# Moving a layer's second expert choice into the next window, and making the samples' input projections with the prompt's weight tiles

## What is computed

```python
mod = (silu(c) @ w_ada + b_ada)                    # 6 x 1024 per sequence
h = rms_norm(x, norm1_g) * (1 + sc1) + sh1
qa, ka, va, qb, kb, vb, zb, bb, ab, qc, kc, vc = split_cols(h @ w_in, IN_SPLITS)   # 1024 x 3592
o_a = window attention (three dilations);  o_b = gated DeltaNet with a causal conv over qb, kb, vb
o_c = stick-breaking attention (samples: over a paged cache)
x = x + gt1 * (concat(o_a, o_b, o_c) @ w_out)
h2 = rms_norm(x, norm2_g) * (1 + sc2) + sh2
q = (h2 @ wq); s = scores against 128 + 128 product keys, 8 heads
top 16 of each half, top 16 of the 256 sums -> 128 experts and gates per token
x = x + gt2 * sum over the 128 experts of gate * gelu(h2 . u_tab[i]) * v_tab[i]
```

## Time and profile before

| | us |
|---|---|
| median of three runs | 4719.75 (4712.13 to 4724.38) |
| profiled execution, its own time | 4694.12 |
| its span in the profile | 4692.3 |
| PE, DVE, ACT, POOL busy | 3425.7, 2843.8, 877.2, 2587.5 |
| moved by DMA | 1401.71 MB, 1107.44 of it by POOL's gathers |

### The profile page before, as it was taken

One profiled execution on the slowest core, in us unless ns is written; L12 is line 12 of the kernel. 1 busy time (PEld: TensorE's weight loads), 2 busy tenths in 40 slices (PEclk: granted clock), 3 DMA queues, 4 the chain that ended last, 5 costly groups with the idle time before them and its releaser, 6 DMA issues. The chain is left out here.

```text
span 4692.3 us, 42307 instructions
## 1 busy us (share of the span) xinstructions
PE 3425.7 (73%) x11982; PEld 1910.2 (41%) x11982; DVE 2843.8 (61%) x5777; ACT 877.2 (19%) x2045; POOL 2587.5 (55%) x2244
## 2 busy tenths in 40 slices
PE   5966768539298889575887967498898436748897
PEld 2624543126154554262455426255553113213351
DVE  1225552556866648787774688868649767584322
ACT  1113110011142112112321211242221011000120
POOL 0000362025767757687774667777656767665563
PEclk8986789759589999796998988799999767869896
DMA  6451375549989989899998889999988989999995
GB/s 229 139 180 56 101 227 177 187 104 320 354 318 345 385 308 339 331 399 342 366 376 320 306 334 395 353 346 361 367 306 308 378 303 348 362 382 377 336 330 154
DMA packets 586674, 1401.71 MB, mean 299 GB/s; under 512 B 67314, under 2 KB 287659, under 8 KB 585244
## 3 DMA queue, kind: packets, MB, share of 16 engines
q0 software_dynamic: 306176, 1107.44, 63.6%
q1 hardware_dynamic: 261836, 274.77, 17.7%
q10 hardware_dynamic: 18432, 16.79, 1.1%
HBM read 1387.11 MB, written 11.88 MB: 298 GB/s over the span
## 5 line engine op out<-in xcount | busy, mean ns | idle before, releaser
L2496 PE MATMUL bank<-arena 128*128 128x512 f32 (+1 forms) x3264 | 1589.6, 636 | 200.5 <-PEq L2493 117.9
L2392 POOL DMA_INDIRECT arena<-in_peer_u_dram,arena x1056 | 1279.6, 1212 | 693.2 <-issue 303.1
L2392 POOL DMA_INDIRECT arena<-in_peer_v_dram,arena x1056 | 1160.5, 1099 | 749.2 <-PE bank L2496 448.4
L2442 DVE CUSTOM_DVE_ANT_0 arena<-arena 128x1024 f32<-128x1024 f32 (+1 forms) x1056 | 1269.8, 1224 | 447.5 <-DMA arena<-in_peer_u_dram,arena 417.4
L2496 PEld LDWEIGHTS bank<-arena 128*128 128x128 f32 (+1 forms) x3264 | 614.8, 196 | 1013.6 <-issue 869.5
L2479 ACT ACTIVATE arena<-arena 128x128 f32<-128x128 f32 (+1 forms) x816 | 301.5, 394 | 1072.9 <-PE bank L2496 686.1
L2458 DVE SCALAR_TENSOR_TENSOR arena<-arena 128x1024 f32<-128x1024 f32 x232 | 297.6, 1283 | 243.6 <-DMA arena<-in_peer_v_dram,arena 223.3
L799 PE MATMUL bank<-arena 128*128 128x256 f32 (+3 forms) x1472 | 368.9, 414 | 101.0 <-PEq L792 95.9
L2138 POOL DMA_INDIRECT arena<-in_cache_sb_k_dram,arena x64 | 84.0, 1312 | 550.4 <-POOLq L2131 530.2
L799 PEld LDWEIGHTS bank<-arena 128*128 128x128 f32 (+1 forms) x1472 | 247.0, 170 | 220.8 <-issue 156.1
L641 PE MATMUL bank<-arena 128*9 128x512 f32 x384 | 180.3, 627 | 66.9 <-PEq L637 45.9
(11 more groups left out here) (339 smaller groups left out, 3730.0 us busy)
## 6 DMA issues: line engine op xcount, KB each, us to landing
arena<-in_w_in_dram SPq DMA_DIRECT2D x78, 1024.0 KB, 13.2
arena<-in_w_ada_dram SPq DMA_DIRECT2D x24, 2048.0 KB, 8.4
arena<-in_w_out_dram SPq DMA_DIRECT2D x24, 1024.0 KB, 13.0
arena<-in_peer_wq_dram SPq DMA_DIRECT2D x24, 1024.0 KB, 15.0
arena<-in_peer_u_dram,arena POOLq DMA_INDIRECT x1056, 7.4
arena<-in_peer_v_dram,arena POOLq DMA_INDIRECT x1056, 6.2
arena<-in_cache_sb_k_dram SPq DMA_DIRECT2D x128, 128.0 KB
arena<-in_cache_sb_v_dram SPq DMA_DIRECT2D x128, 128.0 KB
```

Source lines behind the costliest of these rows:

```text
L2392: pool_.indirect_dma_start(G_[g % GR][0:b.parts, :], None, tables[0 if which == "u" else 1], bass.IndirectOffsetOnAxis(ap=b.index[:, n:n + ...
L2442: vec.tensor_tensor_reduce(row, row, b.h, 1.0, 0.0, ALU.mult, ALU.add, b.AV[0:b.parts, n:n + 1]).then_inc(freed_by_dve, 1)
L2496: last = pe_.matmul(ps[6 + i][0:b.rows, :], DG[owners[g][1] % NDG][0:b.parts, 0:b.rows], G_[g % GR][0:b.parts, i * GBLK:(i + 1) * GBLK], s ...
```

## The change

1. The second `choose_tile` of each unit leaves the lane. It becomes a program of its own, `second_choice`, in the next window at positions 0 to 0.22, that is, in front of the u blocks of tile b. With it gone, layer 1's modulation is no longer in two halves: 24 chunks of 256 columns (tiles of 1 MB, a ring of four) stand beside the one choice left, which is paced 80 there and 59 elsewhere.
2. In a window's last value phase, where v blocks have no u blocks beside them, DVE takes every second row from row 8 on (`ON_DVE_ALONE = 2`): 60 of 128. Elsewhere it stays at one in four.
3. The samples have no projection of their own. The prompt's `project` takes the eight sample rows along: the convolution's matmuls are 264 columns wide in place of 256, and each of the eight other tiles gets a group of eight matmuls for the samples. Layer 0's go with unit 0 straight to the samples' buffers. Layer 1's go with unit 3, in the fourth window, by way of small stores to a DRAM tensor, from where `rows_back` fetches them in the last window; the convolution's features wait in the tile H2S. The samples' norm stands at the head of the sample lane (layer 0) or of the prompt lane (layer 1).
4. In the first window the samples' lane is the norm at positions 0 to 0.02, the rest of layer 0's modulation at 0.02 to 0.25, and from 0.255 the other stages, behind a wait for the prompt's projection. In the last window it spans 0 to 0.8 in place of 0.85. `delta_sample` has three ticks more, in which PE transposes the features to rows for the output.

```diff
+ON_DVE_ALONE = 2
...
-    return not b.sample and n >= FIRST_ON_DVE and n % ON_DVE == ON_DVE - 1
+    return not b.sample and n >= FIRST_ON_DVE and n % b.every == b.every - 1
...
+            for phase in phases:
+                for which, b in phase:
+                    if which == "v":
+                        b.every = ON_DVE_ALONE if len(phase) == 1 else ON_DVE
...
-            def project(u, m):
+            def project(u, m, s=None):
...
-                        mine = [(c, kind, i) for i in range(nt)]
+                        mine = [(c, kind, i) for i in range(nt)] + ([(c, kind, "sample")] if s else [])
...
+                        if spill and t - 2 in of_samples:
+                            k = of_samples.index(t - 2)
+                            lo, hi, _ = CHUNKS[groups[t - 2][0]]
+                            sp_.wait_ge(act2sp, 1).then_inc(act2sp, -1)
+                            sp_.dma_start(ROWS[:, lo:hi], s.m.STAGE[k % 3][:, 0:hi - lo]).then_inc(k_landed[k % 3], 16)
...
-                                    last = pe_.matmul(ps[t % BANKS][:, 0:n_], m.W[c % ring][:, k, off:off + P], m.HT[:, k, 0:n_],
+                                    last = pe_.matmul(ps[t % BANKS][:, 0:wide], m.W[c % ring][:, k, off:off + P], m.HT[:, k, 0:wide],
                                                       start=(k == 0), stop=(k == KD - 1))
+                                elif i == "sample":
+                                    last = pe_.matmul(ps[t % BANKS][0:NB, 0:hi - lo], m.HT[:, k, n_:wide],
+                                                      m.W[c % ring][:, k, 0:hi - lo], start=(k == 0), stop=(k == KD - 1))
...
                                 act_.copy(m.BT[:, f, 3:3 + n_], bank[:, 0:n_]).then_inc(act2dve, 1)
+                                if s is not None:
+                                    act_.copy(s.m.BF[:, f, :], bank[:, n_:wide])
...
+                                if out_to_dram and k >= 3:
+                                    act_.wait_ge(k_landed[k % 3], 16).then_inc(k_landed[k % 3], -16)
...
+                        if spill and t == ticks - 1:
+                            for k in range(len(of_samples) - 3, len(of_samples)):
+                                act_.wait_ge(k_landed[k % 3], 16).then_inc(k_landed[k % 3], -16)
...
+            def rows_back(u, m):
+
+                def sp():
+                    for dst, lo, hi in ((m.PZ[0:NB, 0, :], 2304, 2816), (m.BA[0:NB, 0, :], 2816, 2824), (m.QKC[0:NB, 0, :], 2824, 3336),
+                                        (m.VC[0:NB, 0, :], 3336, 3592), (m.QKA[0:NB, 0, :], 0, 512), (m.VA[0:NB, 0, :], 512, 768)):
+                        sp_.dma_start(dst, ROWS[:, lo:hi]).then_inc(loaded, 16)
+                    yield
+                    sp_.wait_ge(loaded, 96).then_inc(loaded, -96)
+                    yield
...
-                    return [paced(begin, 8), paced(project(u, m), 80), paced(heads(u, m), 14)] + between + [paced(delta_sample(u, m), 75),
+                    return [paced(heads(u, m), 14), paced(delta_sample(u, m), 80),
...
-                return [paced(begin, 14), paced(project(u, m), 102), paced(unit_lengths(u, m), 31), paced(heads(u, m), 19),
+                begin = norm(u, 0, m.H1, m.HT, m.SEG, m.SQJ, m.SMALL, first_w)
+                before = [paced(sample_norm(s.u, m, m.HT), 8)] if s is not None and s.normed is None else []
+                return before + [paced(begin, 14), paced(project(u, m, s), 120 if s else 102), paced(unit_lengths(u, m), 31), paced(heads(u, m), 19),
...
-                        paced(choose_tile(u, e, 0, meanwhile[0:1]), 59), paced(choose_tile(u, e, 1, meanwhile[1:2]), 59)]
+                        paced(choose_tile(u, e, 0, meanwhile), 80 if meanwhile else 59)]
...
+        def second_choice(u, span):
+
+            ticks, programs = LC.choose_tile(u, None, 1)
+            return [span[0] + (span[1] - span[0]) * (n + 1) / ticks for n in range(ticks)], programs
...
-        tiles = [AR.room(KD, GBLK) for _ in range(2)]
-        late = [LP.modulate(1, tiles, GBLK, half * MOD // 2, (half + 1) * MOD // 2) for half in range(2)]
+        late = [LP.modulate(1, [AR.room(KD, GBLK // 2) for _ in range(4)], GBLK // 2)]
...
+        rest_of_samples = [paced(LS.after_lane(LP, LP.walked + 2), 2)] + LS.token_mixers(samples[0], rooms[0])
+        window(LP.token_mixers(units[0], m, own, late),
+               [([paced(LS.sample_norm(samples[0], rooms[0][0], m.HT), 8)], 0.0, 0.02), ([paced(rest, 50)], 0.02, 0.25), (rest_of_samples, 0.255, 1.0)], [])
...
+            choice = second_choice(u, (0.0, 0.22))
             if k < 3:
-                window(LP.token_mixers(units[k + 1]), [], phases)
+                own = None
+                if k == 2:
+                    own = Room()
+                    own.u, own.m, own.normed = samples[1], rooms[1][0], None
+                window(LP.token_mixers(units[k + 1], prompt_room(units[k + 1]), own), [], phases, choice)
...
+                of_sample = [paced(LS.rows_back(samples[1], rooms[1][0]), 4)] + LS.token_mixers(samples[1], rooms[1])
+                window([], [(of_sample, 0.0, 0.8)], phases + [[("u", s)], [("v", s)]], choice)
```

More of the change, by code:

```diff
@@ L163 @@
 ON_DVE = 4
+W_IN = 3592
+ON_DVE_ALONE = 2
 FIRST_ON_DVE = 8
@@ L485, in sample_room @@
             m.DB = AR.room(CONV_CH)
+            m.BF = AR.room(CC, NB) if u.l == 0 else H2S[:, 0:CC * NB].rearrange("p (c b) -> p c b", c=CC)
+            m.STAGE = None if u.l == 0 else [H2S[0:NB, CC * NB + i * (CW_ + 8):CC * NB + (i + 1) * (CW_ + 8)] for i in range(3)]
             rest = AR.at
-            m.HT = AR.room(KD, NB)
-            m.W = [AR.room(KD, CW_ + 8) for _ in range(4)]
             ends = [AR.at]
@@ L745, in project @@
                 tap = {i: f for f, i in feature_at.items()}
-                BANKS = 2 if u.sample else 4
+                of_samples = [i for i, g in enumerate(groups) if g[2] == "sample"]
+                spill = s is not None and s.m.STAGE is not None
+                BANKS = 4
                 ring = len(m.W)
                 ticks = len(groups) + 3
-                T = None if u.sample else m.TMP
+                T = m.TMP
                 def destinations(g):
@@ L782, in pe @@
                     for t in range(ticks):
-                        if t == 0 and not u.sample:
+                        if t == 0:
+                            if s is not None and s.normed is not None:
+                                pe_.wait_ge(*s.normed)
                             pe_.wait_ge(loaded, 16).then_inc(loaded, -16)
@@ L808, in act @@
                         g = t - 1
-                        if g == 0 and not u.sample:
+                        if g == 0:
                             act_.wait_ge(dve2act, 1).then_inc(dve2act, -1)
@@ L839, in dve @@
                                 vec.tensor_copy(m.BT[:, :, 0:3], TAIL).then_inc(dve2act, 1)
-                        if t == 1 and not u.sample:
+                        if t == 1:
                             vec.wait_ge(pe2dve, 1).then_inc(pe2dve, -1)
@@ L1808, in delta_sample @@
                 base = 12
+                ahead = 3
                 ticks = base + 8 + 3
                 def sp():
-                    for t in range(ticks):
-                        if t == 0:
+                    for t in range(-ahead, ticks):
+                        if t == -ahead:
                             sp_.dma_start(m.CWR, ins["conv_w"][l].rearrange("j (c p) -> (j c) p", p=P)).then_inc(loaded, 16)
@@ L1841, in pe @@
                 def pe():
-                    for t in range(ticks):
+                    for t in range(-ahead, ticks):
+                        if t in (-3, -1):
+                            if t == -1:
+                                pe_.wait_ge(act2pe, 1).then_inc(act2pe, -1)
+                            for c in range(8) if t == -3 else range(8, CC):
+                                last = pe_.transpose(ps[c // 4 % 2][0:NB, c % 4 * P:(c % 4 + 1) * P], m.BF[:, c, :], ident)
+                            last.then_inc(pe2act, 1)
                         if t == 1:
                             pe_.wait_ge(loaded, 32).then_inc(loaded, -32)
-                            for c in range(CC):
-                                pe_.transpose(ps[0][:, c * 8:c * 8 + 8], m.DB[0:NB, c * P:(c + 1) * P], ident[0:NB, 0:NB])
+                            pe_.wait_ge(act2pe, 1).then_inc(act2pe, -1)
                             for c in range(CC):
```

98 lines of the change are left out of this document (64 added, 34 removed).

## The result

The changed kernel is slower: 4738.62 us median of 14 runs, against 4710.18 of 14 runs of the kernel before; ratio 1.0059, 95% interval 1.0042 to 1.0076. Its profiled span is 4740.9 us, 49 longer than before.

A forecast was written before the change was run, and what follows sets the result against it. After the first window DMA is the nearest limit, with DVE or PE beside it by stage; waits bound the first. Windows -35 - 3 + 22 + 36 - 37 = -17 on 4694 give 4677, 4702 on the median's scale; range 4605 to 4785.

The forecast's parts named there:

- slower: the choice doesn't fit beside the dot products: Rival, norm and projection: DVE works at 0.906, last value phases of middle windows gain nothing; +43, 4763 us; chance 0.23.
- DVE's needs: Norm and projection of the third, fourth and second window: DVE needs 222, 236 and 199.5 us with the choice moved in.
- I divide DVE's need by it: All stages: need over DVE's best share, 0.945, gives time; third and fourth window's projections 235 and 249 us, +49 and +75.
- The second window: Projection taken as 240 us (+20), next stages +36, output projection to queries +4, choice -63; sum -3.
- The choice at the end: Middle windows' ends: one choice with 31 of 62 rows on DVE takes 99 us where two took 162; -63, -62, -63.
- The last value phase: Last window's end: 128 gathers at 1.33 plus 18 for the samples' queries make 188 us against 226, -38.
- PE loses 30 x 1.76 = 53 us: Last value phase: 30 more rows on DVE take 53 us off PE and add 39 to DVE.
- the middle phase: Last window's middle phase: keeps its bytes at 0.99 of DMA, so 0 change.
- the first phase: Last window's first phase: DVE needs 227 us, over 0.945 is 240 against 239, +1.
- They bring nothing: Last window: the 14 MB of samples' weights no longer loaded free DMA where DVE is the limit, so no gain.
- The first window: Merged projection -10, choice and modulation gone from the middle -39, tail +14: sum -35 (-75 to +10).
- The rival on POOL: Last value phase: gathers at 1.35 plus 0.30 issue keep 128 from going under 211 us; 4725 us; chance 0.08.

The follow-up runs named there:

- e1: The changed kernel with every fourth row on DVE again in the lone value phases; choice still moved, samples still merged: 4750.67 us, 1.0073 of the kernel before.
- e3: The changed kernel with choice and rows as before, leaving the samples' merged projections and the first window's new order: 4666.26 us, 0.9900 of the kernel before.
- e2: The changed kernel with the second choice at the end of its lane again; half rows and merged samples stay: 4728.05 us, 1.0029 of the kernel before.
- e5: e3 with an empty stage of length 84 in the last window's samples' lane, so later stages stand where they did before the change: 4692.61 us.
- e6: e5 with the 14 weight tiles of layer 1's samples loaded in that stage, into room that nothing reads: 4731.22 us.

## Why the prediction was wrong

It said faster, 4702; the rival *slower: the choice doesn't fit beside the dot products* had the mechanism in the third and fourth window, with 4763. That its total came near is partly luck: like the forecast it has the second window at -3, and the last at +2, where -29 was measured.

- **DVE's needs** were right: 222, 236 and 199.5 us foretold for the three projections, 223.07, 234.48 and 197.77 measured. **What failed is the step from need to time**: "I divide DVE's need by it", by 0.945, and in the second window by setting the result against the gathers. The share holds in the bulk of the third window's projection (0.949 in e1), but I gave it to the whole stretch; with the ends, where the gathers start late and the lane's work is out, it is 0.90, in the fourth window 0.865 and in the last one's first phase 0.88. So +57 and +91 (from 191 and 180 us) in place of +49 and +75.
- **The second window**, -3 foretold and +38 measured, holds most of the error. I set DVE's 211 us against 236 of gathers over the whole projection and took 240; it is 270. But it begins with the samples' rows, and behind them DVE stands twice in the changed kernel: 17.0 us for the first prompt block and 19.1 us for the last of the samples' rows on PE. Most of the choice lies behind both, beside dot products. The stretch from output projection to queries also took 25 us more, where +4 was said (20 if before is cut at the last drain too, 166 us against 186).
- **The choice at the end** was right: for the second, third and fourth window -63, -63 and -62 said, -64, -62 and -64 found by the forecast's cuts. Those cut the choices of before up to 5 us early; from the last drain ahead of them they take 155, 157 and 153 us, which makes -59, -57 and -62. DVE is late there, as said.
- **The last value phase**: 188 said, 198 measured, and mainly for another reason. "PE loses 30 x 1.76 = 53 us" by the half rows: PE lost 33 between e3 and e2, since the rows that stay take longer, and the phase 3 (8 between e1 and the changed kernel, 206 to 198). What shortened it, by 30 between e5 and e3, is that the samples' stages moved out of it. The same took 25 us off the middle phase (482 to 457), for which 0 was said; that the last window's sum came near, -37 and -29, is luck, as these 25 cover what the first phase costs.
- **"They bring nothing"**, of the 14 MB: they bring 39 us where the choice isn't in the way (e6 against e5). In the changed kernel that gain is eaten: the first phase went from 245 to 270 us, not +1, with DVE busy 237.71 of them; e3, where the choice isn't there, has 224, and DVE 185.13.
- **The first window**: -35 said, -41 measured, but on balance none of it from the samples (e3: 937 against 938). It is the choice that left: e1 against e3 has -47.
- **The rival on POOL**: gathers in the last value phase take 1.07 us against 1.00 in e1 (137.86 and 129.42 for 129), which agrees with the Trainium skill (SBUF — State Buffer, Who interferes with whom): DVE has 93 us in place of 56 there, for the rows with two SBUF inputs. That the shared interface is the cause was not shown, as DMA's share rose too, from 0.94 to 0.97. It did not decide the phase, which got shorter, 206 to 198.

## What to carry to other kernels

Work that hides at the end of a lane is free only where it stands; before it is moved, see which engine sets the time in the new place. A stretch is not one pool of time: an engine's need is to be set against the part of it in which the engine can work, without its start, its end, and the waits that shut out all that is queued behind. Test the parts of a change alone: here one part won 45 us and the two others lost 72.
